# The context loaded behind the eighth batch of modulation weights, and the first key chunks taken tile by tile

## The chip, the cores and the metric

The kernel runs on one core of one Trainium2 chip. The metric is the device time of one execution in microseconds; the lower the better.

## What is computed

A two-layer hybrid backbone over 512 latent tokens and 256 context tokens of width 2048. Only the opening of layer 0 matters here. For the latent rows `x` and the context rows `ctx` it computes

```
shift, scale, gate = split(silu(c) @ w_mod + b_mod)        # and the same with c_ctx
h  = rmsnorm(x, norm_g)   * (1 + scale)   + shift          # 512 tokens
hc = rmsnorm(ctx, norm_g) * (1 + scale_c) + shift_c        # 256 tokens
k, v   = h  @ w_in[:, keys], h  @ w_in[:, values]
kc, vc = hc @ w_in[:, keys], hc @ w_in[:, values]
```

Windowed attention with the context as prefix, Fourier mixing, the gated output projection, then a pooling layer and a final norm follow; the change leaves them alone.

## The kernel before

All activations stand transposed: 16 tiles of 128 channels by the tokens (`main` for x, `ctx_t` for the context). Every product is in three matmuls of rounded high and low parts (`three`: high x high, high x low, low x high), so weights and activations are both split: ScalarE casts the high part (`hi`, line 427, for weights; `split`, line 450, for tiles), VectorE subtracts for the low part (`lo`, line 781, and `split`, line 855). Line 1300 is the helper in which every matmul is issued.

The opening interleaves three streams of work on TensorE, in a loop over steps k = 0 to 33 (line 1403 on):

- `modulate(k)`, k up to 31: a batch of 1 MB of `mod0` (shift and scale weights) against the conditions. Four batches give one pair of channel tiles; there are eight pairs. SyncE's queue loads batch k into one of three slots when batch k - 3 has been used (`mod_used`). After each fourth batch ScalarE copies the rows (`copy_rows(p)`, line 482) and TensorE turns them (`turn_rows(p)`, in the steps `TURN_STEPS`); then VectorE forms the pair's modulation and gains (`modulation(p)`), and `split_pair(p, v)` norms and splits the two tiles of the latent (v = 0) or the context (v = 1).
- `key_chunk(index)`: 32 chunks, four for each of eight weight units (one unit goes with one pair). A chunk is one of four output banks m, over the two tiles of the unit. It needs the unit's low part (`lo_ready`) and both tiles' low parts (`split_done`). `KEY_STEPS` says which step runs how many: `opening_steps(start, counts, steady, total)` reads `counts` from step `start` on, then `steady` a step. Key units are loaded on GpSimd's queue into the one buffer `key_raw`; unit u waits for the low part of unit u - 1, and `cond_row` (1 MB, used at pair 4) is issued right behind unit 2.
- `context_chunk(index)`: the same for the context's tokens from step 11 on, into other banks, with the same split weights. After the fourth chunk of a unit its weights are free (`weights_used`), and ScalarE may cast the unit after next into their place.

The norms need sums of squares over channels: ScalarE squares tile by tile, VectorE adds the squares (lines 929 for x, 964 for the context), and one matmul with ones sums over partitions (`sum_tokens`, at steps 1 and 8); then `variance` (a reciprocal, line 843) and `root` (line 443). The context is one 2 MB transfer on GpSimd's queue (line 386), issued when three batches have been used.

Order on VectorE: x's adds, variance 1, modulation 0, `split_pair(0, 0)` (with the low part of weight unit 0 inside), the context's 15 adds, modulation 1, `split_pair(1, 0)` (with unit 1), variance 2, the context's first two pairs, then pair after pair. ScalarE follows the same order, with its casts.

Of the kernel before, what the change touches and what calls it, by code (L numbers as in the profile page):

```python
# [24 lines left out]
P = 128  # L25
D = 2048
SEQ = 512
CTX = 256
KT = D // P
GROUP = 4  # L30
# [43 lines left out]

EARLY = KT - GROUP

SQ_X, SQ_C, SQ_0, SQ_1 = starts(KT, KT, KT)

SUM_0, SUM_1, SUM_END = starts(2 + KT, 2 + KT - GROUP)

# [67 lines left out]
    return steps  # L148

KEY_STEPS = opening_steps(6, (1,) * 8 + (0, 1, 1, 1, 1, 1, 1, 0), 1, GROUP * HALVES)
CONTEXT_STEPS = opening_steps(11, (2, 2, 2, 2, 0), 1, GROUP * HALVES)
TURN_STEPS = [3] + [4 * p + 4 for p in range(1, PAIRS)]
SUM_X_STEP, SUM_C_STEP = 1, 8
CONTEXT_SLOTS = 8

SPLIT_ORDER = [(0, 0), (1, 0), (0, 1), (1, 1)] + [(p, v) for p in range(2, PAIRS) for v in range(2)]
# [15 lines left out]
def build(nc, mod0, weights, modb, cond_in, xT, ctxT, vectors, wf, ident_in, identb_in, masks_in, rope_in, dft_tok_in,  # L174
          dft_ch_in, edges_in, outT):
    with ExitStack() as whole:
# [85 lines left out]
        ctx_t = kv_part(k_keys, [KT, CTX])  # L262
        rstd_x = kv_part(k_kc, [SEQ])
        rstd_c = kv_part(k_kc + SEQ, [CTX])

        mod_rows = kvmem[:, k_vc:k_vc + COLS]
        cond_cols = kv_part(k_vc + COLS, [KT, 32])
# [66 lines left out]
        def context_square(j):  # L334

            slot = (j - 1) % CONTEXT_SLOTS
            home = (tmp if slot < 4 else rope)[:].rearrange("p a n -> p (a n)")
            return home[:, slot % 4 * CTX:slot % 4 * CTX + CTX] if j else rstd_c

        block = whole.enter_context(nc.Block())  # L340

# [1 line left out]
        @block.sync  # L343
        def _(sp):
            def load(src, slot):
                sp.dma_start(raw[:, slot].rearrange("p a n -> p (a n)"), src).then_inc(raw_landed[slot], 16)

            def load_batch(k):
                for r in range(2):
                    slot = 2 * (k % BATCH_SLOTS) + r  # L350
                    landed = raw_landed[slot] if slot < RAW_SLOTS else batch_landed[slot - RAW_SLOTS]
                    sp.dma_start(mod_units[slot].rearrange("p a n -> p (a n)"), mod0[2 * k + r]).then_inc(landed, 16)

            for q in range(4):
                sp.dma_start(main[:, 4 * q:4 * q + 4].rearrange("p t n -> p (t n)"), xT[q]).then_inc(x_landed[q], 16)  # L355
            for k in range(BATCHES):
                if k >= BATCH_SLOTS:
                    sp.wait_ge(mod_used, k + 1 - BATCH_SLOTS)
                load_batch(k)
            for j in range(RAW_SLOTS):  # L360
                sp.wait_ge(mod_used, BATCHES - 1 + j // 2)
                load(weights[HALVES + j], j)
            with sp.Fori(1, (G_END - 1) * HALVES // RAW_SLOTS) as q:
                for j in range(RAW_SLOTS):
                    sp.wait_ge(lo_ready, q * RAW_SLOTS + (HALVES + j + 1 - RAW_SLOTS))
                    load(weights[q * RAW_SLOTS + (HALVES + j)], j)
            for t in range(len(LATE_POOL_TILES), KT):
                sp.wait_ge(out_ready, t + 1 - len(LATE_POOL_TILES))
                sp.dma_start(outT[t], main[:, t]).then_inc(stored, 16)
            sp.wait_ge(stored, 16 * (KT - len(LATE_POOL_TILES)))  # L370

        @block.gpsimd
        def _(pool):
            def load(src, slot):
                pool.dma_start(modchunk[:, slot], src).then_inc(chunk_landed[slot], 16)  # L376

            def load_keys(u):
                if u:
                    pool.wait_ge(lo_ready, u)  # L380
                pool.dma_start(key_raw.rearrange("p a n -> p (a n)"), weights[u]).then_inc(key_landed, 16)

            pool.wait_ge(x_landed[3], 16)
            load_keys(0)
            pool.wait_ge(mod_used, 3)
            pool.dma_start(ctx_t.rearrange("p t n -> p (t n)"), ctxT).then_inc(ctx_landed, 16)
            load_keys(1)
            for u in range(2, HALVES):
                load_keys(u)
                if u == 2:  # L390
                    pool.dma_start(cond_row[:], cond_in).then_inc(cond_row_landed, 16)
            pool.dma_start(rope[:], rope_in).then_inc(rope_landed, 16)
            pool.dma_start(edges[:], edges_in).then_inc(rope_landed, 16)
            pool.wait_ge(lo_ready, HALVES)
            pool.dma_start(ident, ident_in).then_inc(attn_landed, 16)
            pool.dma_start(identb, identb_in).then_inc(attn_landed, 16)
            pool.dma_start(masks, masks_in).then_inc(attn_landed, 16)
            pool.wait_ge(mod_used, BATCHES)
            for j in range(2):
                load(modb[j], j)  # L400
            with pool.Fori(1, M_END * HALVES // 2) as q:
                for j in range(2):
                    pool.wait_ge(acc_step, q * 2 + (j - 1))
                    load(modb[q * 2 + j], j)
            for k, t in enumerate(LATE_POOL_TILES):
                if k == 0:
                    pool.wait_ge(gained, len(LATE_POOL_TILES))
                    pool.wait_ge(root_copied, 1)
                nc.gpsimd.tensor_tensor(main[:, t], main[:, t], rstd[:], ALU.mult).then_inc(pool_out, 1)
# [3 lines left out]
        def _(act):  # L413
# [20 lines left out]
            def square_context(j):  # L434
                if j == 0:
                    act.wait_ge(ctx_landed, 16)
                if j > CONTEXT_SLOTS:
                    act.wait_ge(ctx_added, j - CONTEXT_SLOTS)
                nc.scalar.activation(context_square(j), ctx_t[:, j], ACT.Square).then_inc(squared, 1)

            def root(k, dst):
                act.wait_ge(var_ready, k)
# [47 lines left out]
            for t in range(KT):  # L490
                if t % 4 == 0:
                    act.wait_ge(x_landed[t // 4], 16)
                square(t)
            copy_rows(0)
            nc.scalar.activation(stat[:, 0, 0:1], vec[:, V_G0:V_G0 + 1], ACT.Sqrt, scale=0.0)
            root(1, rstd_x)
            hi(G_K, 0, free=False)
            split_pair(0, 0)
            for j in range(KT):
                square_context(j)  # L500
            copy_rows(1)
            hi(G_K, 1, free=False)
            split_pair(1, 0)
            root(2, rstd_c)
            split_pair(0, 1)
            split_pair(1, 1)
# [267 lines left out]
        def _(dve):  # L774
# [172 lines left out]
            def split_pair(p, v):  # L947
                x, rstd_v, hi_part, lo_part = ((main, rstd_x, h_hi, h_lo), (ctx_t, rstd_c, hc_hi, hc_lo))[v]
                for t in (2 * p, 2 * p + 1):
                    normed(x[:, t], x[:, t], gain[:, v, t:t + 1], rstd_v)  # L950
                if v == 0:
                    lo(G_K, p)
                for r in range(2):
                    t = 2 * p + r
                    split(H_X + split_at(p, v) + r, x[:, t], hi_part[:, t], lo_part[:, t], mod0_v[:, 0, t, v:v + 1])

            modulation(0)
            dve.wait_ge(rstd_ready, 1)
            split_pair(0, 0)
            for j in range(1, KT):  # L960
                dve.wait_ge(squared, SQ_C + j + 1)
                if j > 1:
                    dve.wait_ge(ctx_added, j - 1)
                nc.vector.tensor_tensor(rstd_c, rstd_c, context_square(j), ALU.add).then_inc(ctx_added, 1)
            modulation(1)
            split_pair(1, 0)
            dve.wait_ge(tokens_summed, 2)
            variance(2, ps[:, 5, 0:CTX], rstd_c, CTX)
            dve.wait_ge(rstd_ready, 2)
# [328 lines left out]
        def _(pe):  # L1298
# [52 lines left out]
                        beside(s)  # L1351

            def sum_tokens(added, bank, squares, n):
                pe.wait_ge(added, KT - 1)
                mm(ps[:, bank, 0:n], ones, squares, True, True).then_inc(tokens_summed, 1)

            def turn_rows(p):
                pe.wait_ge(rows_ready, p + 1)
# [5 lines left out]
            def modulate(k):  # L1365
# [9 lines left out]
                             mod_units[slot][:, i % 2], b == 0, b == GROUP - 1)  # L1375
                ins.then_inc(mod_used, 1)

            def key_chunk(index):
                u, m = divmod(index, GROUP)
                if m == 0:  # L1380
                    pe.wait_ge(lo_ready, u + 1)
                    pe.wait_ge(split_done, split_at(u, 0) + 2)
                if index == 0:
                    pe.wait_ge(var_ready, 1)
                ins = unit_bank(u, m, BANKS[B_K][m])
                if u == HALVES - 1:
                    ins.then_inc(bank_done, 1)
# [15 lines left out]
            for k, (key_part, context_part) in enumerate(zip(KEY_STEPS, CONTEXT_STEPS)):  # L1403
                if k < BATCHES:
                    modulate(k)
                if k == SUM_X_STEP:
                    sum_tokens(sq_summed, 0, rstd_x, SEQ)
                if k == SUM_C_STEP:
                    sum_tokens(ctx_added, 5, rstd_c, CTX)
                if k in TURN_STEPS and k < BATCHES:  # L1410
                    turn_rows(TURN_STEPS.index(k))
                for index in key_part:
                    key_chunk(index)
                    if k == BATCHES and index == key_part[0]:
                        turn_rows(PAIRS - 1)
                for index in context_part:
                    context_chunk(index)

# [330 lines left out]
```

## Time and profile before

| | |
| --- | --- |
| median of 3 runs | 1464.69 us (1464.18 to 1465.35) |
| profiled execution | 1463.71 us, of which the span from the first to the last instruction is 1462.0 us |
| TensorE matmul busy | 1419.2 us, 97% of the span |
| VectorE, ScalarE, GpSimd busy | 890.0, 498.1, 80.9 us |
| chain that ended last | TensorE 93%, VectorE 4%, DMA 2% |
| mean granted TensorE clock | 0.993 |

The table says which engine is full and which engine's work released the end. An engine that is busy 97% of the time can only be helped by less work or by filling the remaining 3%. In the rows below times are in microseconds from the first instruction; "x8" is the number of instructions merged in a row, and the bracket is the idle time before it and what ended it. A batch, `modulate(k)`, shows as matmuls `ps<-raw,kvmem` or `ps<-modchunk,kvmem` (by slot), eight of them, or as two rows of four where its halves came apart; a key chunk as `ps<-h_hi,w_hi` and its like.

### The profile page before, as it was taken

What the parts mean: (1) busy time and instruction counts of PE and PEld (TensorE: products, weight loads), DVE (VectorE), ACT (ScalarE), POOL (GpSimd) and SP (SyncE); (2) the same over time, 40 slices, a digit from 0 to 9 for tenths busy, and PEclk for the clock granted to TensorE, in tenths of its full rate; (3) what the DMA queues carried; (4) which work ended last, traced back from release to release, by engine and by line L of the source; (5) the groups of instructions that cost most, each with busy time, mean ns of one, the idle gap of its engine ahead of it and who ended that gap; (6) DMA issues with size and microseconds to landing.
All of it is one profiled execution on the core that took longest, in us unless ns stands there. A gap on an engine that the chain in (4) does not pass through costs nothing.

```text
span 1462.0 us, 18260 instructions
## 1 busy us (share of the span) xinstructions
PE 1419.2 (97%) x6822; PEld 1157.9 (79%) x6822; DVE 890.0 (61%) x1389; ACT 498.1 (34%) x733; POOL 80.9 (6%) x151
## 2 busy tenths in 40 slices
PE   4999999999999999999999999999999999999996
PEld 0567888888888888878888888888888888888885
DVE  5554556446767777776566676754555666674433
ACT  5333322234555434354322332211351323332221
POOL 0001111100100000000010110000000000010001
PEclk9999999999999999999999999999999999999998
DMA  9996467556721333324565665332233232366323
GB/s 386 391 360 224 156 204 262 185 171 191 227 74 58 101 116 102 114 72 143 192 195 190 199 200 177 129 101 91 97 101 94 94 101 87 102 201 188 101 73 115
DMA packets 63940, 232.57 MB, mean 159 GB/s; under 512 B 7104, under 2 KB 8000, under 8 KB 62592
## 3 DMA queue, kind: packets, MB, share of 16 engines
q1 hardware_dynamic: 41472, 149.96, 30.7%
q0 software_dynamic: 20144, 75.18, 15.8%
q10 hardware_dynamic: 2256, 6.48, 1.3%
q8 instruction: 47, 0.77, 0.2%
q14 instruction: 21, 0.17, 0.0%
HBM read 227.40 MB, written 4.19 MB: 158 GB/s over the span
## 4 chain that ended last, share of the span: by engine, by line
PE 93%; DVE 4%; DMA 2%; issue 1%; ACT 0%; SPq 0%; DVEq 0%
PE ps L1300 91%; DMA raw<-in_mod 2%; PE ps L1512 2%; DVE w_lo L781 1%; DVE tmp L903 1%; DVE main L1293 1%; DVE main L906 0%; DVE stat L1048 0%; DVE pt_lo L1079 0%; ACT scratch L532 0%; DVE h_lo L853 0%; DVE modchunk L788 0%; ACT w_hi L427 0%; DVE tmp L1085 0%; SPq L355 0%
## 5 line engine op out<-in xcount | busy, mean ns | idle before, releaser
L1300 PE MATMUL ps<-h_hi,w_hi 128*128 128x512 f32 x1600 | 632.4, 395 | 2.8 <-DVE tmp L903 2.2
L1300 PE MATMUL ps<-h_hi,w_lo 128*128 128x512 f32 x1600 | 623.4, 390 | 0.0
L1300 PE MATMUL ps<-h_lo,w_hi 128*128 128x512 f32 x1600 | 622.9, 389 | 0.0
L781 DVE TENSOR_TENSOR w_lo<-raw,w_hi 128x1024 fp32r<-128x1024 f32 x208 | 254.6, 1224 | 372.9 <-ACT w_hi L427 372.7
L427 ACT CAST w_hi<-raw 128x1024 fp32r<-128x1024 f32 x208 | 218.3, 1049 | 650.5 <-PE ps L1300 650.3
L1300 PEld LDWEIGHTS ps<-h_hi,w_hi 128*128 128x128 f32 x1600 | 300.4, 188 | 79.2 <-issue 17.7
L1300 PEld LDWEIGHTS ps<-h_hi,w_lo 128*128 128x128 f32 x1600 | 300.3, 188 | 63.7
L1300 PEld LDWEIGHTS ps<-h_lo,w_hi 128*128 128x128 f32 x1600 | 300.7, 188 | 58.6 <-issue 0.2
L788 DVE CUSTOM_DVE_ANT_0 modchunk<-modchunk,cond_row 128x1024 f32<-128x1024 f32 x128 | 154.7, 1220 | 15.8 <-DMA modchunk<-in_modb 15.8
L376 POOL DMA_DIRECT2D modchunk<-in_modb x128 | 67.6, 528 | 1147.0 <-DVE modacc L788 1122.7
L641 ACT CAST pt_hi<-ps 128x512 fp32r<-128x512 f32 (+1 forms) x48 | 30.7, 639 | 130.3 <-PE ps L1512 130.3
L1048 DVE TENSOR_REDUCE stat<-ps 128x1 f32<-128x513 f32 (+1 forms) x48 | 36.4, 758 | 40.2 <-PE ps L1300 39.9
L1212 DVE SCALAR_TENSOR_TENSOR ubuf<-raw,modv,ubuf 128x512 f32<-128x512 f32 x60 | 45.0, 749 | 2.0 <-DVE ubuf L1234 0.9
L1300 PE MATMUL ps<-raw,kvmem 128*32 128x512 f32 x176 | 29.4, 642 | 15.8 <-DMA raw<-in_mod 15.7
L1079 DVE TENSOR_TENSOR pt_lo<-ps,pt_hi 128x512 fp32r<-128x512 f32 (+1 forms) x48 | 36.1, 753 | 2.6 <-ACT pt_hi L641 2.4
L1300 PE MATMUL ps<-k_hi,q_hi 128*128 128x256 f32 (+1 forms) x96 | 32.2, 336 | 0.0
L1300 PE MATMUL ps<-k_lo,q_hi 128*128 128x256 f32 (+1 forms) x96 | 28.4, 296 | 0.0
L1300 PE MATMUL ps<-k_hi,q_lo 128*128 128x256 f32 (+1 forms) x96 | 28.2, 294 | 0.0
L881 DVE SCALAR_TENSOR_TENSOR main<-ps,modv,main 128x512 f32<-128x512 f32 x32 | 22.2, 745 | 9.1 <-PE ps L1300 9.1
L1300 PEld LDWEIGHTS ps<-raw,kvmem 128*32 128x32 f32 x176 | 4.2, 111 | 27.6 <-issue 16.5
L1060 DVE TENSOR_SCALAR main<-ps 128x384 f32<-128x384 f32 (+1 forms) x16 | 8.9, 558 | 27.5 <-PE ps L1300 27.5
L1300 PE MATMUL ps<-p_hi,w_hi 128*128 128x512 f32 x64 | 25.2, 394 | 0.0
(202 smaller groups left out, 1360.3 us busy)
## 6 DMA issues: line engine op xcount, KB each, us to landing
raw<-in_weights SPq DMA_DIRECT2D x208, 512.0 KB, 3.5
modchunk<-in_modb POOLq DMA_DIRECT2D x128, 512.0 KB, 4.4
raw<-in_mod SPq DMA_DIRECT2D x44, 512.0 KB, 6.3
modchunk<-in_mod SPq DMA_DIRECT2D x20, 512.0 KB, 6.4
main<-in_xT SPq DMA_DIRECT2D x4, 1024.0 KB, 8.3
kvmem<-in_weights POOLq DMA_DIRECT2D x8, 512.0 KB, 6.4
main<-in_xT ACTq DMA_DIRECT2D x4, 1024.0 KB, 4.8
out<-main SPq DMA_DIRECT2D x12, 256.0 KB, 3.1
```

Source lines behind the costliest of these rows:

```text
L376: pool.dma_start(modchunk[:, slot], src).then_inc(chunk_landed[slot], 16)
L427: nc.scalar.copy(w_hi[:, j % 2], src).then_inc(hi_ready, 1)
L641: nc.scalar.copy(*turned_tiles(k - 1, pt_hi)).then_inc(pt_hi_ready, 1)
L781: nc.vector.tensor_tensor(w_lo[:, j % 2], src, w_hi[:, j % 2].bitcast(F32), ALU.subtract).then_inc(lo_ready, 1)
L788: nc.vector.tensor_tensor_reduce(out=modchunk[:, half], in0=modchunk[:, half], in1=cond_row[:, half * (D // 2):(half + 1) * (D // 2)], sca ...
L881: nc.vector.scalar_tensor_tensor(out=main[:, t], in0=ps[:, BANKS[b][m]], scalar=modv[:, layer_gate, t:t + 1], in1=main[:, t], op0=ALU.mult ...
L903: nc.vector.scalar_tensor_tensor(out=t, in0=t, scalar=1.0, in1=ps[:, m], op0=ALU.add, op1=ALU.mult).then_inc(bank_free, 1)
L1048: chain.link(nc.vector.tensor_reduce(stat[:, 0, par:par + 1], ps_flat[:, S_END - width:S_END], AX.X, ALU.max))
L1079: nc.vector.tensor_tensor(lo_part, turned_part, hi_part.bitcast(F32), ALU.subtract).then_inc(pt_ready, 1)
L1212: ins = nc.vector.scalar_tensor_tensor(out=bias_acc[g % 2], in0=raw[:, j % RAW_SLOTS, r], scalar=shift, in1=bias_acc[g % 2], op0=ALU.mult, ...
L1300: return nc.tensor.matmul(out, lhsT, rhs, start=start, stop=stop, skip_group_check=True)
L1512: ins = nc.tensor.transpose(ps_flat[:, 6 * 512 + t * P:6 * 512 + (t + 1) * P], probs[k % 2][:, t * P:(t + 1) * P], ident)
```

## The change

The context's load moves from GpSimd's queue to SyncE's, behind the eighth batch (k = 7). Its tiles are squared two at a time (8 squares of 512 columns for 16 of 256), VectorE adds the 512 wide squares (7 adds for 15), into `sum_c`, and the sum over partitions is two matmuls into the same columns, in step 9 and no longer in step 8. The squares use four places for eight.

Key chunks begin in step 5 and no longer in step 6; three run in step 7, none in steps 11 to 13 and 18. For the first two units a chunk is no more one bank over two tiles, but one tile into two banks (`unit_part`), so that it waits for one tile only. Turn 1 moves from step 8 into step 7, behind that step's first chunk.

On ScalarE the table load and the cast of unit 0 go ahead of `copy_rows(0)`; the cast of unit 1, `copy_rows(1)` and the first high parts of pair 1 go ahead of the context's squares. On VectorE the low part of unit 0 goes ahead of modulation 0, the low part of unit 1 behind `split_pair(0, 0)`, and modulation 1 with `split_pair(1, 0)` ahead of the context's adds. As GpSimd's key loads wait for these low parts, their times move with them.

```diff
-SQ_X, SQ_C, SQ_0, SQ_1 = starts(KT, KT, KT)
+SQ_X, SQ_C, SQ_0, SQ_1 = starts(KT, PAIRS, KT)
...
-KEY_STEPS = opening_steps(6, (1,) * 8 + (0, 1, 1, 1, 1, 1, 1, 0), 1, GROUP * HALVES)
+KEY_STEPS = opening_steps(5, (1, 1, 3, 1, 1, 1, 0, 0, 0, 1, 1, 1, 1, 0, 1, 1, 0), 1, GROUP * HALVES)
 CONTEXT_STEPS = opening_steps(11, (2, 2, 2, 2, 0), 1, GROUP * HALVES)
-TURN_STEPS = [3] + [4 * p + 4 for p in range(1, PAIRS)]
-SUM_X_STEP, SUM_C_STEP = 1, 8
-CONTEXT_SLOTS = 8
+TURN_STEPS = [3, 7] + [4 * p + 4 for p in range(2, PAIRS)]
+SUM_X_STEP, SUM_C_STEP = 1, 9
+CONTEXT_SLOTS = 4
+BY_TILES = 2
...
+        sum_c = kv_part(k_kc + SEQ, [2 * CTX])
...
             slot = (j - 1) % CONTEXT_SLOTS
-            home = (tmp if slot < 4 else rope)[:].rearrange("p a n -> p (a n)")
-            return home[:, slot % 4 * CTX:slot % 4 * CTX + CTX] if j else rstd_c
+            return (tmp, rope)[slot // 2][:, slot % 2, 0:2 * CTX] if j else sum_c
...
                 load_batch(k)
+                if k == 2 * GROUP - 1:
+                    sp.dma_start(ctx_t.rearrange("p t n -> p (t n)"), ctxT).then_inc(ctx_landed, 16)
...
             load_keys(0)
-            pool.wait_ge(mod_used, 3)
-            pool.dma_start(ctx_t.rearrange("p t n -> p (t n)"), ctxT).then_inc(ctx_landed, 16)
             load_keys(1)
...
-                nc.scalar.activation(context_square(j), ctx_t[:, j], ACT.Square).then_inc(squared, 1)
+                nc.scalar.activation(context_square(j), ctx_t[:, 2 * j:2 * j + 2].rearrange("p t n -> p (t n)"),
+                                     ACT.Square).then_inc(squared, 1)
...
+            nc.scalar.activation(stat[:, 0, 0:1], vec[:, V_G0:V_G0 + 1], ACT.Sqrt, scale=0.0)
+            hi(G_K, 0, free=False)
             copy_rows(0)
-            nc.scalar.activation(stat[:, 0, 0:1], vec[:, V_G0:V_G0 + 1], ACT.Sqrt, scale=0.0)
             root(1, rstd_x)
-            hi(G_K, 0, free=False)
             split_pair(0, 0)
-            for j in range(KT):
+            hi(G_K, 1, free=False)
+            copy_rows(1)
+            split_pair(1, 0)
+            for j in range(PAIRS):
                 square_context(j)
-            copy_rows(1)
-            hi(G_K, 1, free=False)
-            split_pair(1, 0)
             root(2, rstd_c)
...
-                if v == 0:
+                if v == 0 and p >= BY_TILES:
                     lo(G_K, p)
...
+            lo(G_K, 0)
             modulation(0)
             dve.wait_ge(rstd_ready, 1)
             split_pair(0, 0)
-            for j in range(1, KT):
+            lo(G_K, 1)
+            modulation(1)
+            split_pair(1, 0)
+            for j in range(1, PAIRS):
                 dve.wait_ge(squared, SQ_C + j + 1)
                 if j > 1:
                     dve.wait_ge(ctx_added, j - 1)
-                nc.vector.tensor_tensor(rstd_c, rstd_c, context_square(j), ALU.add).then_inc(ctx_added, 1)
-            modulation(1)
-            split_pair(1, 0)
+                nc.vector.tensor_tensor(sum_c, sum_c, context_square(j), ALU.add).then_inc(ctx_added, 1)
...
+            def sum_context():
+                pe.wait_ge(ctx_added, PAIRS - 1)
+                mm(ps[:, 5, 0:CTX], ones, sum_c[:, 0:CTX], True, False)
+                mm(ps[:, 5, 0:CTX], ones, sum_c[:, CTX:], False, True).then_inc(tokens_summed, 1)
...
+            def unit_part(u, r, half):
+
+                for m in (2 * half, 2 * half + 1):
+                    cols = slice(m * P, (m + 1) * P)
+                    three(ps[:, BANKS[B_K][m]], w_hi[:, u, r, cols], w_lo[:, u, r, cols],
+                          h_hi[:, 2 * u + r], h_lo[:, 2 * u + r], u == 0 and r == 0, False)
...
                 if index == 0:
                     pe.wait_ge(var_ready, 1)
+                if u < BY_TILES:
+                    if m % 2 == 0:
+                        pe.wait_ge(split_done, split_at(u, 0) + m // 2 + 1)
+                    unit_part(u, m // 2, m % 2)
+                    return
+                if m == 0:
+                    pe.wait_ge(split_done, split_at(u, 0) + 2)
...
-                if k in TURN_STEPS and k < BATCHES:
+                if k in TURN_STEPS and k != TURN_STEPS[1] and k < BATCHES:
                     turn_rows(TURN_STEPS.index(k))
                 for index in key_part:
                     key_chunk(index)
-                    if k == BATCHES and index == key_part[0]:
-                        turn_rows(PAIRS - 1)
+                    if k in (TURN_STEPS[1], BATCHES) and index == key_part[0]:
+                        turn_rows(TURN_STEPS.index(k))
```

## Rows read from the trace of the kernel before

**Rows 1.** Busy time by stretch, opening; last columns: granted clock, DMA share, GB/s
```profile
0.00:20.00 20.00, 4.81 (x16) 0.74 (x16) 11.17 (x22) 11.57 (x20) 0.93 (x5) 1.00 0.90 362
20.00:40.00 20.00, 13.70 (x52) 2.67 (x50) 12.41 (x19) 10.00 (x23) 1.06 (x2) 0.83 1.02 414
40.00:60.00 20.00, 20.00 (x117) 11.11 (x115) 12.78 (x25) 5.63 (x10) 1.05 (x2) 1.00 1.01 398
60.00:80.00 20.00, 20.00 (x135) 13.25 (x134) 11.65 (x24) 7.12 (x11) 1.05 (x2) 1.00 0.99 374
```

**Rows 2.** The chain that ended last: start, length, what
```profile
18.56 6.58 DMA raw<-in_mod
...
26.65 12.36 DMA raw<-in_mod
...
39.05 366.63 PE ps L1300 x1832
```

**Rows 3.** Timeline of TensorE: the batches of steps 4, 5, 8 to 13
```profile
27.91 1.06 PE L1300 MATMUL ps<-raw,kvmem 128*32 128x512 f32 x8
32.04 1.71 PE L1300 MATMUL ps<-modchunk,kvmem 128*32 128x512 f32 x4 [3.07 <-DMA modchunk<-in_mod]
35.21 1.92 PE L1300 MATMUL ps<-modchunk,kvmem 128*32 128x512 f32 x4 [1.46 <-DMA modchunk<-in_mod]
...
44.22 1.77 PE L1300 MATMUL ps<-modchunk,kvmem 128*32 128x512 f32 x8
45.92 0.70 PE L1300 MATMUL ps<-kvmem,ones_r 128*128 128x256 f32 x2
...
48.83 1.06 PE L1300 MATMUL ps<-raw,kvmem 128*32 128x512 f32 x8
...
51.41 1.06 PE L1300 MATMUL ps<-raw,kvmem 128*32 128x512 f32 x8
...
58.01 1.07 PE L1300 MATMUL ps<-raw,kvmem 128*32 128x512 f32 x8
...
62.89 1.07 PE L1300 MATMUL ps<-raw,kvmem 128*32 128x512 f32 x8
```

**Rows 4.** DMA issues of the opening: KB each, median us to landing
```profile
kvmem<-in_ctxT POOLq DMA_DIRECT2D x1, 2048.0 KB, 10.7
cond_row<-in_cond POOLq DMA_DIRECT2D x1, 1024.0 KB, 9.9
```

**Rows 5.** Timeline of GpSimd: context, third key unit, cond_row
```profile
24.01 0.53 POOL L386 DMA_DIRECT2D kvmem<-in_ctxT  x1 [9.36 <-PE ps L1300]
...
50.76 0.53 POOL L381 DMA_DIRECT2D kvmem<-in_weights  x1 [18.36 <-DVE w_lo L781]
51.27 0.53 POOL L391 DMA_DIRECT2D cond_row<-in_cond  x1
```

**Rows 6.** Groups of instructions by form: busy, mean ns of one
```profile
L846 DVE SCALAR_TENSOR_TENSOR main<-main,gain,kvmem 128x512 f32<-128x512 f32 x16 | 11.3, 749 | 0.8 <-ACT kvmem L443 0.6
...
L929 DVE TENSOR_TENSOR kvmem<-kvmem,tmp 128x512 f32<-128x512 f32 x15 | 10.4, 693 | 2.4 <-ACT tmp L432 1.0
...
L432 ACT ACTIVATE tmp<-main 128x512 f32<-128x512 f32 x15 | 9.3, 628 | 2.3 <-DVE kvmem L929 2.0
...
L846 DVE SCALAR_TENSOR_TENSOR kvmem<-kvmem,gain 128x256 f32<-128x256 f32 x16 | 7.0, 480 | 0.5 <-ACT kvmem L443 0.5
...
L843 DVE RECIPROCAL kvmem<-scratch 128x256 f32<-128x256 f32 x1 | 1.8, 1753 | 0.0
```

**Rows 7.** Timelines of ScalarE and VectorE: unit 2 cast, its tiles' low parts
```profile
63.05 1.04 ACT L427 CAST w_hi<-kvmem 128x1024 fp32r<-128x1024 f32 x1 [4.90 <-PE ps L1300]
...
65.27 1.41 DVE L855 SCALAR_TENSOR_TENSOR h_lo<-main,mod_v,h_hi 128x512 fp32r<-128x512 f32 x2
```

**Rows 8.** Busy time by stretch around the clock's fall
```profile
31.00:32.00 1.00, 0.00 (x0) 0.00 (x0) 1.00 (x2) 0.20 (x1) 0.13 (x1) 1.00 0.92 389
32.00:33.00 1.00, 0.96 (x4) 0.14 (x4) 0.90 (x2) 0.00 (x0) 0.40 (x1) 0.65 0.84 352
```

More of the change, by code:

```diff
@@ L1351, in group, with sum_x @@
                         beside(s)
-            def sum_tokens(added, bank, squares, n):
-                pe.wait_ge(added, KT - 1)
-                mm(ps[:, bank, 0:n], ones, squares, True, True).then_inc(tokens_summed, 1)
+            def sum_x():
+                pe.wait_ge(sq_summed, KT - 1)
+                mm(ps[:, 0], ones, rstd_x, True, True).then_inc(tokens_summed, 1)
+            def sum_context():
+                pe.wait_ge(ctx_added, PAIRS - 1)
+                mm(ps[:, 5, 0:CTX], ones, sum_c[:, 0:CTX], True, False)
+                mm(ps[:, 5, 0:CTX], ones, sum_c[:, CTX:], False, True).then_inc(tokens_summed, 1)
             def turn_rows(p):
@@ L1381, in key_chunk @@
                     pe.wait_ge(lo_ready, u + 1)
-                    pe.wait_ge(split_done, split_at(u, 0) + 2)
                 if index == 0:
                     pe.wait_ge(var_ready, 1)
+                if u < BY_TILES:
[5 more added lines that the diff above has]
+                    pe.wait_ge(split_done, split_at(u, 0) + 2)
                 ins = unit_bank(u, m, BANKS[B_K][m])
@@ L1406, in _ @@
                 if k == SUM_X_STEP:
-                    sum_tokens(sq_summed, 0, rstd_x, SEQ)
+                    sum_x()
                 if k == SUM_C_STEP:
-                    sum_tokens(ctx_added, 5, rstd_c, CTX)
-                if k in TURN_STEPS and k < BATCHES:
+                    sum_context()
+                if k in TURN_STEPS and k != TURN_STEPS[1] and k < BATCHES:
                     turn_rows(TURN_STEPS.index(k))
```

## The prediction

> **What bounds the kernel now.** I read first the table of stretches [rows 1]. It shows two regimes: up to 40 us TensorE works only in part (13.70 busy of 20 between 20 and 40) while the DMA share stands at 1.02; from 40 us on TensorE is busy throughout, with the DMA share still at 1.01 and 0.99. The chain that ended last [rows 2] says the same: until 39.05 us it is mostly mod0 transfers, the last from 26.65, and then 366 us of TensorE without a break. So the only time that an edit in the opening can give back is what TensorE idles before it runs gapless, and what it must not do is to open a new gap later. The TensorE timeline [rows 3] places the gaps: step 4 starts at 27.91, step 5 gets its halves at 32.04 and 35.21, the second half of step 6 comes at 39.05 [rows 2], and the batch of step 8 takes from 44.22 on 1.77 us where the others take 1.06: its second half came late, near 44.9. After 46 us the steps follow one another without a hole: 48.83, 51.41, then 58.01 and 62.89 for steps 12 and 13. The late batches are late because the context's 2 MB were issued at 24.01 [rows 5] and took 10.7 us to land [rows 4], in the same stretch.
>
> **What the change does to the transfers.** By 40 us 362 x 20 + 414 x 20 = 15.5 MB have moved [rows 1]. Take the context (2.10 MB, 5.1 us at 414 GB/s) from before batches 5 to 7 and put it behind batch 7: steps 5, 6 and 7 come about 5 us earlier. From landing to landing a batch of 1.05 MB takes 2.5 us alone; I get step 5 at 29.8 (batch 3 was in at 25.1 [rows 2], two batches follow), step 6 at 33.4 (the second key unit's load is now issued near 27.4, as its release, the low part of unit 0, moves into VectorE's idle time ahead of modulation 0), step 7 at 35.9. For step 8 nothing is gained: the context is in front of it. And something is lost that the diff does not name. The low part of unit 1 used to wait for modulation 1 and the context's sums; now it runs as soon as unit 1 has landed, near 35 us. It releases the third key load and, right behind it, cond_row on GpSimd's queue, which went out at 50.76 and 51.27 [rows 5]. They are 0.52 + 1.05 MB, 3.9 us of the DMA engines, and now run beside the context and ahead of batch 8.
>
> The bytes that must be in for step 8 are x 4.19, vectors 0.12, nine batches 9.44, context 2.10, three key units 1.57, cond_row 1.05: 18.5 MB. That is 3.0 MB over the 15.5 at 40 us: at 398 GB/s, the rate after 40 us [rows 1], 7.4 us, so 47.4; at 414, 47.1. I take 47.3, against the 44.9 of before. In the same way batch 12 can't be in before 57.2 to 57.9 us (22.7 MB). That is the first bound.
>
> The Trainium skill, page DMA: Bandwidth & Descriptors, section "Issuing engines are not separate DMA queues", says that transfers from any issuing engine end on the same 16 DMA engines and interleave; by it the move from GpSimd's queue to SyncE's changes order and not bytes. The 10.7 us of the context beside SyncE's batches agree. A sum that let the context have its own bandwidth would put step 8 at 43 and the gain above 4 us.
>
> **TensorE between.** Key chunks are 1.4 us each in a row, 1.5 behind a batch (51.41 less 48.83 is a step of batch and chunk, 2.58, of which the batch is 1.06 [rows 3]; a chunk stays six matmuls, only their order over tiles and banks changes). Step 5: batch to 30.8, first chunk (tile 0 only, whose low part is there at about 30.8) to 32.2; step 6: 33.4 to 35.9; step 7: batch to 36.9, chunk 2 to 38.4, turn 1 (0.9) to 39.3, chunk 3 to 40.7. Chunk 4 needs tile 2: modulation and gain 0.5, then normed, high and low part at some 0.75 each as the normed row has it [rows 6], with hand-overs 2.9 behind the turn, 42.2; it ends at 43.6. So five chunks and a turn are done before step 8, where before it was two: 4.2 + 0.9 us of work ahead. But then TensorE waits for batch 8 until 46.0 (first half) and 47.3.
>
> From 47.3: batch 8 to 48.3, chunk 5 to 49.9, batch 9 to 50.9. Now sum_context stands in step 9. The context lands at about 44; eight squares of 512 columns (0.63 each) and seven adds at 0.69 [rows 6] plus some 0.08 between them, 5.4 us behind the second square, end at 51.0: the sum starts at 51.1, a wait of 0.2. It is two matmuls where it was one: 0.5 us more (one is 0.70 with its drain [rows 3]). Then to 52.2, chunk 6 to 53.7, batch 10 to 54.7, chunk 7 to 56.2, batch 11 to 57.2. The context's first pair needs the variance with its reciprocal of 1.75, the root, and normed, high and low parts of half width at 0.48 [rows 6], with the hand-overs about 5.0 us behind the sum: 57.2, just in time. Two context chunks 1.5: 58.7. Three halts of a few tenths (batches 9 to 12 land at 49.9, 52.4, 55.2, 57.6) I put at 0.5 together. Step 12 then starts at 59.2, 1.2 us later than the 58.01 of before, but with eight chunks done and not six: 2 x 1.4 = 2.8 us ahead. The net is 1.6 us.
>
> Steps 12 to 18 lose those two chunks. Their cover was also that of unit 2: its weights are free only after step 12, and in the trace of before the low part of its tiles is done about 3.8 us later (TensorE's step 13 begins at 62.89 [rows 3]; the last h_lo of the pair ends at 66.68 [rows 7]). TensorE now has step 13 without a key chunk (1.06 + 1.5) and batch 14 (1.06) in between, 3.4 to 3.6: a wait of 0.4. Fewer instructions elsewhere (8 squares for 16, 7 adds for 15) save ScalarE and VectorE time that no one waits for. Copy_rows, the table load and the casts that change places on ScalarE lie before its wait for the rows and cost nothing; if turn 0 came a little later, TensorE would only wait less for batch 5.
>
> Sum: -2.8 + 1.2 + 0.4 = **-1.2 us**. All behind step 19 is the same work, gapless, and shifts as a block.
>
> **Bounds.** For the best end drop all new waits: step 12 at the byte bound 57.4 and the rest as before, 2.8 + 0.6 = 3.4 us faster. For the worst, rivals 2 and 3.
>
> **Rivals.**
> 1. *Batch 8 comes sooner* (cond_row gives way to SyncE's queue, or the DMA engines hold 430 GB/s): TensorE's new waits go, 2.2 to 3.4 us faster, 1461.9 at 2.8. For it: 414 GB/s held over 20 us before 40 [rows 1], more than the 398 that I reckon with. Against: the byte count leaves 3.4 at most.
> 2. *TensorE's clock falls in the new gap.* The trace shows that it can: between 28.9 and 32.04 TensorE had nothing [rows 3], and right after the granted clock went down (0.65 between 32 and 33 [rows 8]) from 2.4 to 1.2 GHz, and it was back for the stretch from 40 [rows 1]. My gap is 2.4 us (43.6 to 46.0), somewhat shorter, with another of 0.4 behind one half batch. Some 7 us at half clock from 46 on: batch 8 and chunk 5 double (+2.4), partly where the next batch would have been waited for anyway; 1.9 us more, 0.7 slower than before, 1465.4. The Trainium skill, page TensorE: Matmul & The Clock Gate, section "HAM oscillation — how this bites in real kernels", tells of waits for transfers that bring down the clock each time; the trace of before shows one such fall.
> 3. *The context's sum is late* and stands in front of everything on TensorE: chunks 6 and 7 and batches 10 and 11 are queued behind it, and so are loads 13 and 14. If the context's packets are served after cond_row's and it lands at 47.5, squares and adds end at 54.3, 3.2 us behind my 51.1: step 12 at 62.4, 2.0 us slower than before, 1466.7. It decides from 52.3 on: a sum that late eats the 1.2.
> 4. *Nothing moves* because the transfers were the bound throughout: covered, as the forecast holds it in large part.
>
> **How the numbers follow.** The profiled execution took 1463.71 us around a span of 1462.0; the median of the runs is 1464.69, 1.0 above it. I set the change against the median: 1464.69 - 1.2 = 1463.5. Chances: forecast 0.50 (0.6 to 2.0 faster), rival 1 0.27, rival 2 0.15, rival 3 0.08. Measurement tells 0.2% (2.9 us) from no change. Of rival 1 about half reaches 2.9, so faster 0.15; of rival 3 about half, so slower 0.04, rounded up for a gap that I do not see to 0.05; within 0.2% 0.80. The range takes in rival 1 to its byte bound and rival 2: 1461.2 to 1465.8.
>
> **What will show it.** In the profile after: step 5 near 29, TensorE without work for 2 to 3 us before the batch of step 8, that batch at 46 to 47.5; cond_row issued before 40; the context landed at 43 to 45; the context's sum at 51; step 12 at 59; a short wait ahead of chunk 8; gapless from there on. A step 8 before 45, or a granted clock under 1.00 after 44 us, would make the forecast wrong, up or down.

## The result and the profile after

The changed kernel takes 1467.35 us (median of 18 runs, 1466.01 to 1469.39), the kernel before 1464.85 us (18 runs, 1464.18 to 1466.18): 2.5 us slower, a ratio of 1.0018 with a 95% interval from 1.0011 to 1.0025. The forecast was 1463.5, 1.2 us faster, in a range up to 1465.8.

The profiled execution of the changed kernel took 1469.39 us around a span of 1467.7, the longest of its 18. Its table of stretches, with the columns of [rows 1]:

```profile
20.00:40.00 20.00, 18.58 (x88) 6.96 (x84) 10.27 (x12) 6.49 (x9) 1.58 (x3) 1.00 1.04 419
40.00:60.00 20.00, 15.00 (x58) 7.29 (x58) 10.78 (x18) 6.19 (x12) 0.00 (x0) 0.83 0.92 355
60.00:80.00 20.00, 19.74 (x138) 12.68 (x137) 10.56 (x24) 7.53 (x13) 0.53 (x1) 1.00 0.97 342
```

Between 20 and 40 us TensorE has become busy, 18.58 us for 13.70 in [rows 1]. The next stretch gives it back: 15.00 of 20, and there the mean granted clock is 0.83, where it was 0.83 one stretch earlier before. The DMA rate falls to 355 and 342 GB/s, from 398 and 374.

The chain that ended last, in the same stretch as [rows 2] (start, length, what):

```profile
31.84 17.46 DMA modchunk<-in_mod
...
49.35 17.50 PE ps L1304 x90
...
66.92 1.05 ACT w_hi L428
...
68.00 1.23 DVE w_lo L783
69.23 1.33 DVE h_lo L857 x2
...
81.91 8.22 DMA modchunk<-in_mod
...
90.18 49.92 PE ps L1304 x306
```

Where the chain before had left the transfers for good at 39.05, it now rests on the second half of batch 8 until 49.35, then on the cast and the low parts of unit 2 at 66.92, and once more on a transfer, batch 20's second half, until 90.14.

TensorE's timeline, steps 5, 6, 8, 9, 12 and 14, as in [rows 3]:

```profile
29.10 1.05 PE L1304 MATMUL ps<-modchunk,kvmem 128*32 128x512 f32 x4
30.38 1.05 PE L1304 MATMUL ps<-modchunk,kvmem 128*32 128x512 f32 x4 [0.23 <-DMA modchunk<-in_mod]
...
32.94 2.01 PE L1304 MATMUL ps<-raw,kvmem 128*32 128x512 f32 x8
...
43.14 0.47 PE L1304 MATMUL ps<-h_hi,w_hi 128*128 128x512 f32 x1 [1.47 <-DVE h_lo L857]
...
45.90 1.05 PE L1304 MATMUL ps<-modchunk,kvmem 128*32 128x512 f32 x4 [1.14 <-DMA modchunk<-in_mod]
49.35 1.92 PE L1304 MATMUL ps<-modchunk,kvmem 128*32 128x512 f32 x4 [2.39 <-DMA modchunk<-in_mod]
...
54.06 1.62 PE L1304 MATMUL ps<-raw,kvmem 128*32 128x512 f32 x8
55.61 1.13 PE L1304 MATMUL ps<-kvmem,ones_r 128*128 128x256 f32 x4
...
63.26 1.07 PE L1304 MATMUL ps<-raw,kvmem 128*32 128x512 f32 x8
...
70.70 0.47 PE L1304 MATMUL ps<-h_hi,w_hi 128*128 128x512 f32 x1 [0.26 <-DVE h_lo L857]
```

Step 5's batch is done at 31.4 and step 6's at 34.9, for 37 and 40 before: the early part of the gain is there. Then TensorE waits for tile 2 until 43.14, has nothing from about 44.7 to 45.90, and after the first half of batch 8 nothing for 2.39 us more. Step 12 starts at 63.26, for 58.01. With two chunks (2.8 us) more done that is a net loss of 2.4 us at the start of step 12. Its last turn, in step 32, starts at 132.60 for 128.07, so 4.5 us of the 5.7 between the two profiled executions lie in the opening. Most of the rest lies behind the last products, as the last section shows.

GpSimd's timeline and the landings (KB each, us from issue to landing), beside [rows 4, 5]:

```profile
27.80 0.53 POOL L384 DMA_DIRECT2D kvmem<-in_weights  x1 [13.09 <-DVE w_lo L783]
37.36 0.53 POOL L384 DMA_DIRECT2D kvmem<-in_weights  x1 [9.02 <-DVE w_lo L783]
37.88 0.53 POOL L392 DMA_DIRECT2D cond_row<-in_cond  x1
```

```profile
kvmem<-in_ctxT SPq DMA_DIRECT2D x1, 2048.0 KB, 13.1
...
cond_row<-in_cond POOLq DMA_DIRECT2D x1, 1024.0 KB, 11.2
...
modchunk<-in_mod SPq DMA_DIRECT2D x1, 512.0 KB, 17.5
```

Cond_row goes out at 37.88, not at 51.27, and lands 11.2 us later, at 49.1. The context, issued at 29.95, lands at 43.1. The second half of batch 8, issued at 31.84, is 17.5 us on its way, to 49.35.

### The profile page after: what moved, and what is told of

Its sections match the earlier page's. It is cut to its first block, busy times and chain, and to the rows that moved or that the text cites. A ratio compares the mean times of both kernels' runs of the same rounds, so it can differ in the third digit from the quotient of the medians.

```text
span 1467.7 us, 18240 instructions
## 1 busy us (share of the span) xinstructions
PE 1424.7 (97%) x6824; PEld 1161.0 (79%) x6824; DVE 888.4 (61%) x1381; ACT 497.7 (34%) x725; POOL 80.3 (5%) x150
## 3 DMA queue, kind: packets, MB, share of 16 engines
q0 software_dynamic: 20000, 73.08, 15.5%
HBM read 227.40 MB, written 4.19 MB: 158 GB/s over the span
## 4 chain that ended last, share of the span: by engine, by line
PE 91%; DVE 4%; DMA 3%; issue 1%; ACT 0%; SPq 0%; DVEq 0%; ACTq 0%
PE ps L1304 90%; DMA modchunk<-in_mod 2%; PE ps L1534 2%; DVE w_lo L783 1%; DMA raw<-in_mod 1%; DVE tmp L905 1%; DVE main L1297 0%; DVE main L908 0%; DVE stat L1052 0%; ACT w_hi L428 0%; DVE pt_lo L1083 0%; ACT scratch L534 0%; DVE h_lo L855 0%; DVE modchunk L790 0%; DVE tmp L1089 0%
```

## The experiments

Each was timed in five rounds beside the kernel before; the ratio is to that kernel.

**cond_row late.** In the changed kernel:

```diff
                 load_keys(u)
-                if u == 2:
+                if u == 3:
                     pool.dma_start(cond_row[:], cond_in).then_inc(cond_row_landed, 16)
```

> The changed kernel with cond_row's 1 MB issued behind the fourth key unit (near 69 us) and no longer behind the third (37.9). Theory A (the loss comes from the transfers ahead of batch 8: its second half came at 49.35, TensorE waited 3.5 us in all and its clock fell): batch 8 is complete 2 to 2.6 us sooner, near 47, the clock stays up, and step 12 starts near 60 and not at 63.3; 1.5 to 4 us faster than the changed kernel, about 1464.5. Theory B (the loss comes from the order on TensorE: two chunks taken out of steps 11 to 13, the sum as two matmuls, unit 2 waited for): within 0.5 us of the changed kernel's 1467.35.

Measured: 1462.67 us, ratio 0.9986 [0.9977, 0.9995]: 4.7 us faster than the changed kernel, where 1.5 to 4 was expected, and 2.2 faster than the one before. TensorE's timeline and one stretch of the table:

```profile
45.37 2.21 PE L1304 MATMUL ps<-modchunk,kvmem 128*32 128x512 f32 x8 [0.64 <-DMA modchunk<-in_mod]
...
49.09 1.06 PE L1304 MATMUL ps<-raw,kvmem 128*32 128x512 f32 x8
50.09 1.13 PE L1304 MATMUL ps<-kvmem,ones_r 128*128 128x256 f32 x4
...
57.72 1.07 PE L1304 MATMUL ps<-raw,kvmem 128*32 128x512 f32 x8
```

```profile
40.00:60.00 20.00, 17.82 (x99) 9.69 (x99) 13.85 (x25) 8.47 (x16) 0.00 (x0) 1.00 1.01 392
```

The second half of batch 8 is used from 46.53 on (its weight loads start there), step 12 starts at 57.72, and the granted clock is 1.00 in every 20 us stretch up to 140. Batch 8 still comes later than the 44.9 of before. Theory A holds. Theory B falls: the order on TensorE, the doubled sum and the wait for unit 2 are all still in this kernel.

**The gap filled.** In the changed kernel, fill(6) behind step 7's chunks and fill(9) between the halves of batch 8:

```diff
+            def fill(n):
+                for _ in range(n):
+                    mm(ps[:, 4], w_hi[:, 0, 0, 0:P], h_hi[:, 0], True, True)
```

> The changed kernel with 15 matmuls without use (128x512, 0.23 us each) in the gap: 6 behind step 7's work, 9 between the halves of batch 8, into a bank that nothing holds then. It adds work that is not in the reference, and its output is the same. If the fall of the clock carries part of the loss, the granted clock stays at 1.00 through the opening, the matmuls cost nothing as they lie in waits, and the time is 1 to 2 us below the changed kernel, near 1466, with less spread. If the clock is only a companion of the wait and TensorE would have waited for the next batches anyway, the time is that of the changed kernel, within 0.5 us. The wait for batch 8 itself stays at 49.3 in either.

Measured: 1466.14 us, ratio 1.0011 [1.0002, 1.0020]. TensorE's timeline:

```profile
49.40 1.05 PE L1304 MATMUL ps<-modchunk,kvmem 128*32 128x512 f32 x4
...
60.62 1.07 PE L1304 MATMUL ps<-raw,kvmem 128*32 128x512 f32 x8
```

Batch 8's second half comes no sooner, 49.40, but what follows runs at full clock: the batch of step 8 is over in 1.05 where it took 1.92, and step 12 starts 2.6 us earlier than in the changed kernel's profile, at 60.62. The medians differ by 1.2 us only, and the two intervals overlap. The fall of the clock is shown for the profiled execution; that it is worth about 1.2 us in the median is likely, and no more than that. The clocks of all executions point the same way. The mean granted clock over a whole execution averages 0.9937 over the 18 of the changed kernel and 0.9946 over the 11 with the gap filled: 0.0009 of 1467 us, an estimate of 1.3 us. The profiled execution of the changed kernel stands at 0.992, the lowest of its 18 (one other has it), so what its rows show of the fall is more than the typical execution paid.

**The context's load as before.** In the changed kernel:

```diff
-                if k == 2 * GROUP - 1:
-                    sp.dma_start(ctx_t.rearrange("p t n -> p (t n)"), ctxT).then_inc(ctx_landed, 16)
...
             load_keys(0)
+            pool.wait_ge(mod_used, 3)
+            pool.dma_start(ctx_t.rearrange("p t n -> p (t n)"), ctxT).then_inc(ctx_landed, 16)
             load_keys(1)
```

> The changed kernel with the context's load back on GpSimd's queue, when three batches are used (24 us), all else as changed: early chunks, tile by tile, sum in step 9, cond_row behind the third key unit. Theory A: steps 5 and 6 are late as in the kernel before (32 to 39), step 8 is near 47 to 48 as all the same bytes stand ahead of it, but TensorE has waited earlier and has its chunks still to do while batch 8 comes; step 12 near 59 to 61, 1464 to 1466. Theory B: as the changed kernel, 1467.3, or above it.

Measured: 1469.04 us, ratio 1.0028 [1.0019, 1.0037], slower than any other kernel here, where 1464 to 1466 was expected. TensorE's timeline, the first chunk of tile 2, batch 8 and the context's sum:

```profile
48.95 0.47 PE L1304 MATMUL ps<-h_hi,w_hi 128*128 128x512 f32 x1 [1.47 <-DVE h_lo L857]
...
50.51 1.06 PE L1304 MATMUL ps<-modchunk,kvmem 128*32 128x512 f32 x8
...
55.71 1.13 PE L1304 MATMUL ps<-kvmem,ones_r 128*128 128x256 f32 x4 [1.56 <-DVE kvmem L970]
```

Turn 1 waits for batch 7, tile 2 for turn 1 (48.95), and VectorE adds the context's squares only behind pair 1, so the sum on TensorE waits another 1.56 us, until 55.71, though the context, issued at 23.93, took 10.7 us to land. The expectation of its theory A counted transfers and missed this; the time is what theory B named, 1467.3 or above: the new order of ScalarE and VectorE belongs to a late context. Load and order are no separate gains.

**cond_row early in the kernel before.** In the kernel before, its issue moved from behind key unit 2 to behind key unit 1:

```diff
             load_keys(1)
+            pool.dma_start(cond_row[:], cond_in).then_inc(cond_row_landed, 16)
             for u in range(2, HALVES):
                 load_keys(u)
-                if u == 2:
-                    pool.dma_start(cond_row[:], cond_in).then_inc(cond_row_landed, 16)
```

> The kernel before with cond_row issued behind the second key unit (near 32 us) and no longer behind the third (51). If 1 MB ahead of batches 7 and 8 is what costs, step 8 comes some 2.5 us later than 44.2, and the kernel is 1.5 to 2.5 us slower than before, about 1466.9. If its place does not matter, 1464.85 within 0.3.

Measured: 1466.88 us, ratio 1.0016 [1.0007, 1.0025], 2.0 us slower. TensorE's timeline, the second half of step 7, steps 8 and 12:

```profile
44.69 1.05 PE L1299 MATMUL ps<-raw,kvmem 128*32 128x512 f32 x4 [0.78 <-DMA raw<-in_mod]
...
47.27 1.06 PE L1299 MATMUL ps<-modchunk,kvmem 128*32 128x512 f32 x8
...
60.34 1.07 PE L1299 MATMUL ps<-raw,kvmem 128*32 128x512 f32 x8
```

Step 8 at 47.27 is 3.1 us behind the 44.22 of [rows 3]. The 1 MB alone, with nothing else of the change, costs about what the whole change lost.

**cond_row late in the kernel before.** The edit of the first experiment, made in the kernel before.

> The kernel before with cond_row issued behind the fourth key unit (66 us) and no longer behind the third (51). A control for e1_cond_late: if the 2.2 us which that kernel is faster than the kernel before are owed to the change freed of cond_row, this one shows nothing, 1464.85 within 0.3, as TensorE in the kernel before waits for no batch after 46 us. If a later cond_row is worth something by itself, about 1463.

Measured: 1465.27 us, ratio 1.0005 [0.9996, 1.0014], 0.3 above the kernel before in the same rounds (1464.97). No gain: the 2.2 us of the first experiment are the change's own, once cond_row is out of its way.

**Unit 2 late as well.** cond_row late, and:

```diff
             load_keys(1)
+            pool.wait_ge(mod_used, 10)
             for u in range(2, HALVES):
```

> The changed kernel with cond_row behind the fourth key unit, as in e1_cond_late, and the third key unit's load held back until ten batches are used (about 50 us; it is needed near 60). Another 0.52 MB, 1.3 us of the DMA engines, leave the stretch ahead of batch 8. If bytes ahead of batch 8 are what counts, batch 8 is complete near 45.5 and not at 46.6, and the time is 0.7 to 1.3 us below e1_cond_late's 1462.67, near 1461.7. If the chain of the context's sum has taken over as the bound there, the time stays within 0.4 of e1_cond_late.

Measured: 1463.02 us, ratio 0.9989 [0.9980, 0.9998], no better than cond_row late alone. TensorE's timeline, batch 8, the sum, step 12:

```profile
44.68 1.85 PE L1305 MATMUL ps<-modchunk,kvmem 128*32 128x512 f32 x8
...
50.03 1.13 PE L1305 MATMUL ps<-kvmem,ones_r 128*128 128x256 f32 x4 [0.91 <-DVE kvmem L971]
...
57.69 1.06 PE L1305 MATMUL ps<-raw,kvmem 128*32 128x512 f32 x8
```

Batch 8 is over a microsecond sooner, and the time is lost one step later: TensorE waits 0.91 us for VectorE's last add. Step 12 starts at 57.69 for 57.72. Once unit 2 is late too, the context's sum is the next bound, as the second alternative said.

**cond_row behind batch 8 on the same queue.** In the changed kernel, taken from GpSimd's queue and put into SyncE's loop:

```diff
+                if k == 2 * GROUP:
+                    sp.dma_start(cond_row[:], cond_in).then_inc(cond_row_landed, 16)
```

> The changed kernel with cond_row on SyncE's queue, directly behind batch 8, and not on GpSimd's. The bytes up to batch 9 stay as they are, only their place in the order is changed: they cannot share the engines with batch 8 any more. If the halves of batch 8 come late because cond_row is served beside them, batch 8 is complete near 47 and the wait moves to batches 9 to 11; gain over the changed kernel 0.5 to 2 us, 1465.3 to 1466.9. If only the total of bytes counts, in the sense that the 2.6 us come back in full at batch 9, it equals the changed kernel at 1467.35 within 0.5.

Measured: 1465.38 us, ratio 1.0004 [0.9995, 1.0013], 2.0 us below the changed kernel. TensorE's timeline, batches 8 and 9:

```profile
45.53 2.22 PE L1304 MATMUL ps<-modchunk,kvmem 128*32 128x512 f32 x8 [0.64 <-DMA modchunk<-in_mod]
...
50.46 1.05 PE L1304 MATMUL ps<-raw,kvmem 128*32 128x512 f32 x4 [1.12 <-DMA raw<-in_mod]
51.73 1.05 PE L1304 MATMUL ps<-raw,kvmem 128*32 128x512 f32 x4 [0.21 <-DMA raw<-in_mod]
```

Batch 8 comes as in the first experiment, and the second half of batch 9 then at 51.73. The wait is cut in two pieces, 0.64 and 1.12 us before the first halves, and the clock stays up. The same bytes in another order are worth 2 us, the clock's share included.

**Key steps as before.** cond_row late, and the old list of key steps (from step 6 on, one chunk a step):

> e1_cond_late with the old list of key steps (from step 6 on, one a step): the loads and the order of ScalarE and VectorE are as in e1_cond_late, but only two chunks are done ahead of batch 8 and not five. If the gain of the change lies in filling the wait for batch 8, it is gone here: step 8 starts as in e1_cond_late, one chunk more is left up to step 12 and two fewer are done by then, 4.2 us, and the longer gap brings the clock down as well: 1466.9 to 1468.6. If earlier batches alone give the gain, it stays near 1463.

Measured: 1466.67 us, ratio 1.0011 [1.0002, 1.0020], 4.0 us slower than with the new list. TensorE's timeline and one stretch of the table:

```profile
44.44 3.05 PE L1304 MATMUL ps<-modchunk,kvmem 128*32 128x512 f32 x8 [4.19 <-DMA modchunk<-in_mod]
...
59.47 1.07 PE L1304 MATMUL ps<-raw,kvmem 128*32 128x512 f32 x8
```

```profile
46.00:48.00 2.00, 2.00 (x7) 0.50 (x2) 1.78 (x3) 1.19 (x3) 0.00 (x0) 0.50 1.05 420
```

TensorE waits 4.19 us for batch 8, the clock is at 0.50 behind it, and step 12 starts at 59.47 with only six chunks done. Early batches alone give nothing; the gain is the work put into the wait, and the clock which that work keeps up. The two are not separated here: the mean granted clock over the runs is 0.9937, for 0.9948 with the new list. The result is 0.2 under the expected span of 1466.9 to 1468.6.

**Four chunks in step 7.** cond_row late, and the counts of steps 7 and 8 as 4 and 0:

> e1_cond_late with four key chunks in step 7 and none in step 8, so that chunk 5 fills the wait for batch 8 (in e1_cond_late TensorE has 0.6 us of nothing before its first half and about 1 us before its second). If what TensorE has left to do ahead of batch 9 still counts there, 0.5 to 1.3 us below e1_cond_late's 1462.67. If the transfers set the pace at batch 9 as well (1.05 MB behind batch 8, 2.6 us), the filled time is waited for one step later and nothing is gained, within 0.4.

Measured: 1462.87 us, ratio 0.9986 [0.9977, 0.9995]: no gain over 1462.67. TensorE's timeline:

```profile
46.00 1.66 PE L1304 MATMUL ps<-modchunk,kvmem 128*32 128x512 f32 x8
47.88 1.05 PE L1304 MATMUL ps<-raw,kvmem 128*32 128x512 f32 x4 [0.23 <-DMA raw<-in_mod]
49.16 1.05 PE L1304 MATMUL ps<-raw,kvmem 128*32 128x512 f32 x4 [0.23 <-DMA raw<-in_mod]
```

The filled time is waited for at batch 9, whose halves are used as they land, 47.88 and 49.16. The same list with unit 2 late:

> e5_unit2_late (third key unit held back as well) with the same list as e9_four_in_step7. e5_unit2_late waited 0.9 us for the context's sum, and chunk 5 moved ahead lengthens that wait by what it shortens the rest: within 0.5 us of e5_unit2_late's 1463.02. A gain of 1 us or more would say that the sum was no bound.

Measured: 1463.21 us, ratio 0.9987 [0.9978, 0.9996], as expected. No version went below the 1462.67 of cond_row late.

## Why the prediction was wrong

**Steps 5 to 7 were right, within 1.1 us.** Step 5 at 29.8 was 29.10 and 30.38 for its halves, tile 2 at 42.2 was 43.14, the five chunks before step 8 ended near 44.7 (43.6). The early third key unit and cond_row, named as what the diff does not say, went out at 37.4 and 37.9.

**The step that failed: "The bytes that must be in for step 8 ... so 47.4".** The second half of batch 8 was in at 49.35. The count took every byte that had moved as landed. By 49.35 it is 361 x 20 (the first stretch) + 419 x 20 + 402 x 9.35 = 19.4 MB moved, 0.9 MB more than the 18.5 on the list; the last term is this stretch of the changed kernel:

```profile
40.00:49.35 9.35, 4.35 (x19) 2.30 (x18) 7.35 (x13) 5.77 (x10) 0.00 (x0) 0.95 0.99 402
```

The surplus belongs to transfers issued behind batch 8 and still on their way: batches 9 and 10 went out between 34.99 and 39, and the first half of batch 9 was in 1.3 us after batch 8. That it is theirs follows from what had been issued; no view gives the bytes of one transfer. With cond_row late it is the same: 18.2 MB moved by 46.6 for 17.4 needed. These are the stretch of that kernel and the one of the kernel before:

```profile
40.00:46.60 6.60, 4.42 (x20) 2.33 (x21) 5.17 (x10) 5.14 (x9) 0.00 (x0) 1.00 1.00 402
```

```profile
40.00:44.94 4.94, 4.94 (x27) 2.40 (x25) 2.98 (x7) 1.53 (x2) 0.00 (x0) 1.00 1.03 408
```

The kernel before could have told: 15.5 + 408 GB/s over 4.94 us = 17.5 MB by the 44.9 at which its batch 8 landed, for 16.9 needed. An allowance of 0.6 to 0.9 MB, 1.6 to 2.2 us, was missing.

**Rival 2, with 0.15, came true on top.** With batch 8's second half 2 us later there was more of nothing around its first half, 1.14 and 2.39 us for 2.4 and 0.4 forecast, and the clock fell in the profiled execution, the sign that the prediction had named for its own failure. Its stretches around the fall:

```profile
47.50:49.40 1.90, 0.05 (x2) 0.05 (x4) 1.67 (x3) 0.15 (x1) 0.00 (x0) 0.74 1.03 412
49.40:52.00 2.60, 2.60 (x6) 0.84 (x7) 0.69 (x1) 0.00 (x0) 0.00 (x0) 0.50 1.03 406
52.00:54.00 2.00, 2.00 (x5) 1.12 (x4) 0.00 (x0) 0.00 (x0) 0.00 (x0) 0.50 0.95 281
54.00:56.00 2.00, 2.00 (x11) 0.57 (x11) 0.00 (x0) 0.00 (x0) 0.00 (x0) 0.69 0.80 326
56.00:58.00 2.00, 2.00 (x10) 1.44 (x8) 1.19 (x2) 0.00 (x0) 0.00 (x0) 1.00 0.51 131
```

From 49.4 to 54 the clock is 0.50, 1.2 GHz for 2.4. The rival was priced at 1.9 us; the filled gap gives 2.6 in step 12's start and 1.2 in the median.

**A term that was too small: the halts behind step 12.** The forecast had 0.4 us there, for unit 2, and then "all behind step 19 is the same work, gapless". In the profiled execution the last turn lies 4.5 us behind, while the net at step 12 was 2.4. Of the 2.1 between, the wait for unit 2 is 0.26 (70.70), batch 20, whose second half is used at 90.18, costs 1.3, and batch 22 0.4. With cond_row late the same stretch costs 1.1 us (57.72 less 58.01 less 2.8 is -3.1; the last turn at 126.06 for 128.07 is -2.0), with the gap filled 1.3 (-0.2 at step 12, last turn at 129.14).

Batch 20's halt goes with the new list of key steps, which gives step 18 no chunk. The batch can be issued only when batch 17 has been used. That was at 81.54, 7.3 us ahead of its turn at 88.88, where before it was 8.7 (77.36 for 86.08); and its halves took 7.1 and 8.2 us to land, for 4.7 and 6.4. The kernel with the old list and late cond_row, whose clock fell as well, loses nothing in the stretch: 1.5 behind at step 12 and 1.5 at the last turn (129.57). But the list is not all of it. The kernel before with cond_row early, which has the old list too, goes from 2.3 behind to 3.8 (131.89). That the slow clock adds to the halts, because TensorE frees no slot meanwhile (131 GB/s between 56 and 58 in the table above), is possible and not shown.

**Summed for the median:** the forecast is -1.2, and batch 8 was 2.0 later. The kernel with the gap filled, where the clock is out of it, gives the next two terms. From batch 8's second half to step 12 it took 11.2 us (49.40 to 60.62) for 11.9 forecast, -0.7: the wait for the sum and the three halts of the forecast did not come. Behind step 12 it lost 1.3 for 0.4, +0.9. That is +1.0 for this kernel, measured at +1.3. With about 1.2 for the clock the changed kernel comes to 2.2, measured +2.5. The terms from stretches are sized from single profiled executions, the clock from a difference of medians; 0.3 stay open.

**Rival 1 was right in direction, and its size was just reached.** It said that with batch 8 sooner, cond_row giving way, TensorE's new waits would go and the kernel be 2.2 to 3.4 us faster; cond_row late gave 2.2, with 0.64 us and about 1 us of the waits left. It failed as a forecast because nothing in the changed kernel keeps cond_row back. Rival 3 did not occur: the sum started at 55.61, but TensorE came to it only then (adds done by 50.2, batch 9 from 54.06), with no wait. The two waits of the first experiment, ahead of the halves of batch 8, and the halves of batch 9 in the one with four chunks were for transfers. The bytes and not the context's chain set the pace until cond_row and unit 2 were both moved away.

## What to carry to other kernels

A load that waits for another engine's progress moves when that engine's order changes: list all such loads, and the bytes that they put ahead of the next transfer waited for. When landings are worked out from a rate, add what is in flight behind the transfer in question (0.6 to 0.9 MB here, 1.6 to 2.2 us).
```profile
1452.10 2.09 PE ps L1304 x8
```

These eight small matmuls took 1.17 us in the profiled execution before. The granted clock had gone to 0.50 near 1451.2 us, just ahead of them (0.67 between 1449.53 and 1454.53), where before it went down near 1448.8 us, behind them (0.88 between 1445 and 1450). That is 0.9 of the 1.2 us by which this execution is longer behind the opening. It does not go with the change: of the profiled executions that keep the change, those of cond_row behind batch 8, of four chunks in step 7 and of the same with unit 2 late have 1.17, those of the filled gap and of the old key steps 2.09.
